# Score matmuls of two split heads issued together on four row groups, with a fourth score bank taken from the turned probabilities

## Chip, cores, metric

The kernel runs on one core of one Trainium2 chip. The metric is device time in microseconds of one execution: the median of several, compared with the kernel before on the same chip.

## What is computed

A first block (mixed attention, then a hierarchical mixture of experts) is followed by two layers of a second block, over 256 tokens of width 1024 in float32. The change concerns the two layers of the second block. Each projects its normalized input to 24 tiles of 128 columns, does three kinds of attention, gates them, and projects back:

```python
def second_block(x, mem, ...):
    for l in range(2):
        h = rms_norm_2(x, pre_norm[l]); proj = h @ w_in[l]
        # D: 6 "split" heads. Each has two halves of 32 columns with a softmax of their own
        #    p = softmax(q1 k1^T / sqrt(32)) - lam * softmax(q2 k2^T / sqrt(32));  o = p @ v
        # G: 6 heads of 64 columns on 2 key heads (normalized, rotated)
        # M: 4 heads of 64 columns against a memory of 256 rows
        y = concat([rms(o_D) * silu(gate_D), o_G * silu(gate_G), o_M * silu(gate_M)]) @ w_out[l]
        x = x + rms_norm_2(y, post_norm[l])
```

For a D head, a score matrix of 256 x 256 is computed for each half with a contraction of only 32.

## The kernel before

Every engine has a program of its own, written out in one fixed order, and they meet at semaphores. That order comes from `schedule()`: a list of turns, each of which has **jobs** and then at most one attention **step**. Jobs are the pieces beside attention: `tile2` (one 128-column tile of the input projection, 24 matmuls in three passes of a float32 product split in high and low parts, lines 851 to 853), `swap` (the pair exchange of the rotation, L1031), `vn` (a turn of values, L1027), `hsq` and `hso` (sums over a head, L1034, L1038), `y2` (output projection). Steps of a layer are D0 to D5, G0 to G5, M0 to M3.

In the turn of a step TensorE does, in this order: the step's scores (`run_scores`), the turn's jobs, for every second step the product of probabilities and values of two earlier heads (`run_out`, L1192 and L1196), and the turn (transpose) of the probabilities of the step before (`run_turn`, L1145). VectorE normalizes the step before (`norms`), takes the row maxima of this step's scores (`maxes`, L1940 for D, L1946 for G and M), and then makes the low parts of the weights that coming `tile2` jobs use (`low`, L2187) and takes jobs. ScalarE does the exponentials (`exps`, L1515 for D, L1521 for G and M), the high parts of the weights (`high`, L1572), the jobs' results out of PSUM, and the turned probabilities out of PSUM (`take_turned`, L1542). The two steps M2 and M3 at a layer's end have no projection tiles beside them; there the turn of M3's probabilities follows that of M2's.

PSUM has eight banks: score banks 0 to 2 in rotation over score jobs (`n % 3`), banks 3 and 4 in alternation for turned probabilities (`3 + n % 2`), 5 for the products with the values, 6 and 7 for jobs. A D step is two score jobs, one for each half, and so takes two banks; `s_bank(n)` waits until the exponentials of the step that had the bank last are done. A D step's four matmuls (L1104) have 32 rows of the array each: an even head's two halves lie on array rows 0 to 31 and 32 to 63, an odd head's on 64 to 95 and 96 to 127. G and M heads are already scored two at a time, on two groups of 64 rows, in the turn of the even one (L1123).

Of the kernel before, what the change touches and what calls it, by code (L numbers as in the profile page):

```python
# [11 lines left out]
ALU = mybir.AluOpType  # L12
ACT = mybir.ActivationFunctionType
X = mybir.AxisListType.X
# [279 lines left out]


S_OWNER = [n for n, s in enumerate(STEPS) for _ in range(S_JOBS[s[0]])]


def item_of(job):
# [99 lines left out]
def build(nc, ins, out):  # L399
    ctx = ExitStack()  # L400
    with ctx:
# [443 lines left out]
        def _(pe):  # L845
# [196 lines left out]

            def s_bank(n):

                if n >= 3:
                    owner = S_OWNER[n - 3]
                    if STEPS[owner][0] in "AB":
                        pe.wait_ge(maxed, owner + 1)
                    else:
                        pe.wait_ge(exped, owner + 1)  # L1050
                return bank(n % 3)

            def run_scores(step):
                kind, l, h = STEPS[step]
                n = s_first(step)
                if kind == "A":
                    for tile in (h % 2, 2):
                        from_act(("tile1", tile))
                    base = HD * (h // 2)
                    q, k = tile3[base:base + HD, h % 2, :], tile3[base:base + HD, 2, :]  # L1060
                    s = s_bank(n)
                    pe.matmul(s[:, 0:P], q[:, 0:P], k[:, 0:P], start=True, stop=True)
                    pe.matmul(s[:, P:3 * P], q[:, P:T], k[:, 0:T], start=True, stop=True).then_inc(scores, 1)
                elif kind == "C":
                    from_act(("cqt", 3))
                    pe.wait_ge(setup, 2)
                    q, k = qc3[0:C_QK, h, :], kc3[0:C_QK, h, :]
                    s = s_bank(n)
                    pe.matmul(s[:, 0:P], q[:, 0:P], k[:, 0:P], start=True, stop=False)
                    pe.matmul(s[:, 0:P], ident_b[:, :], causal_b[:, :], start=False, stop=True)  # L1070
                    pe.matmul(s[:, P:3 * P], q[:, P:T], k[:, 0:T], start=True, stop=False)
                    pe.matmul(s[:, 2 * P:3 * P], ident_b[:, :], causal_b[:, :], start=False, stop=True
                              ).then_inc(scores, 1)
                elif kind == "B":
                    for g in range(B_GROUPS):
# [12 lines left out]
                    s = s_bank(n + 1)  # L1088
                    for g in range(2):
                        q, k = qk(g)  # L1090
                        mm = pe.matmul(s[:, T * g:T * g + T], q[:, P:T], k[:, 0:T], start=True, stop=True)
                    mm.then_inc(scores, 1)
                    s = s_bank(n + 2)
                    q, k = qk(2)
                    pe.matmul(s[:, 0:T], q[:, P:T], k[:, 0:T], start=True, stop=True).then_inc(scores, 1)
                elif kind == "D":
                    pe.wait_ge(roped, max(rope_nth(l, h // 2), rope_nth(l, 3 + h // 2)))

                    banks = [s_bank(n), s_bank(n + 1)]
                    for tt in range(2):  # L1100
                        for m in range(2):
                            base = HD * (h % 2) + 32 * m
                            q, k = tile3[base:base + 32, h // 2, :], tile3[base:base + 32, 3 + h // 2, :]
                            mm = pe.matmul(banks[m][:, T * tt:T * tt + T], q[:, P * tt:P * tt + P], k,  # L1104
                                           start=True, stop=True)
                            if tt == 1:
                                mm.then_inc(scores, 1)
                elif h % 2 == 0:
                    if kind == "G":
                        pe.wait_ge(k_copied, l + 1)  # L1110
                    else:
                        from_act(("tile2", l, 20 + h // 2))
                    two = []
                    for m in range(2):
                        rows = slice(HD * m, HD * m + HD)
                        if kind == "G":
                            own = 15 if m == (h + m) // 3 else 16
                            two.append((s_bank(n + m), tile3[rows, 12 + h // 2, :], tile3[rows, own, :]))
                        else:
# [270 lines left out]
        def _(act):  # L1390
# [96 lines left out]
            def exps(step):  # L1487
# [15 lines left out]
                    op = act.activation(pr[:, 384:1152], pr[:, 384:1152], ACT.Exp, bias=n_[:, 1:2],  # L1503
                                        accum_out=s_[:, 1:2])
                elif kind == "C":
                    s = bank(b0 % 3)
# [4 lines left out]
                elif kind == "D":  # L1511
                    for m in range(2):
                        for tt in range(2):
                            c = 2 * m + tt
                            op = act.activation(pr[:, T * c:T * c + T], bank((b0 + m) % 3)[:, T * tt:T * tt + T],  # L1515
                                                ACT.Exp, bias=n_[:, c:c + 1], scale=32 ** -0.5,
                                                accum_out=s_[:, c:c + 1])
                else:
                    s = bank(b0 % 3)
# [13 lines left out]
            def take_turned(step):  # L1533
                kind = STEPS[step][0]
                w = 3 * P if kind in "ABC" else 4 * P
                for m in range(T_JOBS[kind]):
                    n = t_first(step) + m
                    if n >= 4:
                        owner = max(s for s in range(len(STEPS)) if t_first(s) <= n - 4)
                        act.wait_ge(o_ready, OUT_OF[owner] + 1)  # L1540
                    act.wait_ge(turned, n + 1)
                    act.activation(probsT[:, 512 * (n % 4):512 * (n % 4) + w], bank(3 + n % 2)[:, 0:w], ACT.Copy  # L1542
                                   ).then_inc(turned_out, 1)

            def inverse_root(dst, src, scale=1.0, bias=0.0):
# [209 lines left out]
        def _(dve):  # L1755
# [140 lines left out]
            def maxes(step):  # L1896
# [11 lines left out]

                if kind == "A":
                    dve.wait_ge(scores, b0 + 1)  # L1910
                    s = bank(b0 % 3)
# [4 lines left out]
                elif kind == "B":  # L1916
                    heads = A_HEADS + h
                    dve.wait_ge(scores, b0 + 1)
                    biased(pr[:, 0:384].rearrange("p (g t) -> p g t", g=3),
                           bank(b0 % 3)[:, 0:384].rearrange("p (g t) -> p g t", g=3),  # L1920
                           bias3[:, heads:BIAS_HEADS:B_HEADS, P - 1::-1], m_[:, 0:1])
                    dve.wait_ge(scores, b0 + 2)
                    biased(pr[:, 384:896].rearrange("p (g t) -> p g t", g=2),
                           bank((b0 + 1) % 3).rearrange("p (g t) -> p g t", g=2),
                           bias3[:, heads:heads + B_HEADS + 1:B_HEADS, ::-1], m_[:, 1:2])
                    dve.wait_ge(scores, b0 + 3)
                    link(biased(pr[:, 896:1152], bank((b0 + 2) % 3)[:, 0:T], bias3[:, heads + 2 * B_HEADS, ::-1],
                                m_[:, 2:3]))
                    link(dve.tensor_tensor(m_[:, 1:2], m_[:, 1:2], m_[:, 2:3], ALU.max))
                    dve.tensor_scalar(n_[:, 0:2], m_[:, 0:2], -1.0, None, ALU.mult).then_inc(maxed, 1)  # L1930
                elif kind == "C":
                    dve.wait_ge(scores, b0 + 1)
                    s = bank(b0 % 3)
                    dve.tensor_reduce(m_[:, 0:1], s[:, 0:P], X, ALU.max)
                    link(dve.tensor_reduce(m_[:, 1:2], s[:, P:3 * P], X, ALU.max))
                    dve.tensor_scalar(n_[:, 0:2], m_[:, 0:2], -(C_QK ** -0.5), None, ALU.mult).then_inc(maxed, 1)
                elif kind == "D":
                    for tt in range(2):
                        dve.wait_ge(scores, b0 + tt + 1)
                        op = dve.tensor_reduce(m_[:, 2 * tt:2 * tt + 2],  # L1940
                                               bank((b0 + tt) % 3).rearrange("p (m t) -> p m t", m=2), X, ALU.max)
                    link(op)
                    dve.tensor_scalar(n_[:, 0:4], m_[:, 0:4], -(32 ** -0.5), None, ALU.mult).then_inc(maxed, 1)
                else:
                    dve.wait_ge(scores, b0 + 1)
                    link(dve.tensor_reduce(m_[:, 0:2], bank(b0 % 3).rearrange("p (m t) -> p m t", m=2), X, ALU.max))  # L1946
# [420 lines left out]
```

## Time and profile before

| | us |
|---|---|
| median of 3 runs (753.81, 754.43, 759.05) | 754.43 |
| the profiled execution, its own time | 761.98 |
| its span from first to last instruction | 760.2 |
| mean granted TensorE clock of it | 0.952 of full speed |

The profile is of one execution, which was longer than the median. Rows give start and length of instructions in microseconds from the span's start. A matmul in float32 (not the split products) shows as two records. The first layer of the second block runs from about 445 us on, the second from about 597 us.

### The profile page before, as it was taken

The numbers are of one execution on the slowest core, as the hardware profiler recorded it, in microseconds if no ns is written. First come the engines' busy times: TensorE is split into PE (matmuls) and PEld (weight loads), VectorE is DVE, ScalarE is ACT, GpSimd is POOL, SyncE is SP. The second block draws the span as 40 slices with busy tenths as digits, with TensorE's granted clock in tenths as the row PEclk, the third lists the DMA queues.
The fourth block names the chain that finished last, engine by engine and source line by source line (L and its number), as shares of the span: only waits on it lengthen the run. The fifth ranks groups of instructions, "written<-read, shape, count | busy, mean of one in ns | idle before, by whom it ended". The sixth has DMA issues, their size and how long they took to land.

```text
span 760.2 us, 11653 instructions
## 1 busy us (share of the span) xinstructions
PE 682.1 (90%) x4580; PEld 520.5 (68%) x4582; DVE 368.4 (48%) x813; ACT 324.3 (43%) x759; POOL 16.8 (2%) x31
## 2 busy tenths in 40 slices
PE   6989999996599999798796799999979999999986
PEld 4968998695343455264251388878859898888876
DVE  1633657445432132021121456678775466787733
ACT  2565665421000112020120243678865545788742
POOL 5001000000000000000000000000000000000000
PEclk9999999898589999898989899999999999999999
DMA  9967331399959999999999729008163080073301
GB/s 280 340 201 246 111 112 56 123 302 367 315 223 350 414 410 414 415 409 416 414 410 411 251 88 300 1 1 274 61 221 111 1 274 5 1 231 103 111 1 56
DMA packets 94616, 167.80 MB, mean 221 GB/s; under 512 B 4238, under 2 KB 75648, under 8 KB 90464
## 3 DMA queue, kind: packets, MB, share of 16 engines
q1 hardware_dynamic: 92272, 160.88, 59.0%
q0 software_dynamic: 2160, 6.07, 2.3%
q8 instruction: 39, 0.64, 0.3%
q14 instruction: 17, 0.14, 0.1%
q10 hardware_dynamic: 128, 0.08, 0.0%
HBM read 165.93 MB, written 1.07 MB: 220 GB/s over the span
## 4 chain that ended last, share of the span: by engine, by line
PE 72%; SPq 11%; DMA 5%; ACT 5%; DVE 4%; issue 2%; ACTq 0%; DVEq 0%
PE psum L851 13%; PE psum L853 11%; PE psum L852 11%; SPq L741 9%; PE psum L1206 4%; PE psum L1247 4%; PE psum L894 4%; PE psum L1145 3%; DMA ring<-in_w_expert_down_dram 3%; PE psum L1261 3%; PE psum L1192 2%; DMA ring<-in_w_expert_up_dram 2%; PE psum L986 2%; PE psum L1104 2%; PE psum L1233 1%
## 5 line engine op out<-in xcount | busy, mean ns | idle before, releaser
L851 PE MATMUL psum<-a_high,w_high 128*128 128x256 f32 x512 | 150.9, 295 | 2.1 <-ACT q_c L1472 1.3
L853 PE MATMUL psum<-a_high,w_low 128*128 128x256 f32 x512 | 144.7, 283 | 0.0
L852 PE MATMUL psum<-x_low,w_high 128*128 128x256 f32 x512 | 144.6, 283 | 0.0
L2187 DVE TENSOR_TENSOR w_low<-ring,w_high 128x1024 fp32r<-128x1024 f32 (+1 forms) x79 | 111.2, 1421 | 23.4 <-ACT w_high L1572 23.3
L851 PEld LDWEIGHTS psum<-a_high,w_high 128*128 128x128 f32 x512 | 97.7, 191 | 13.8 <-issue 4.7
L1572 ACT ACTIVATE w_high<-ring 128x1024 fp32r<-128x1024 f32 (+1 forms) x79 | 95.9, 1219 | 9.6 <-DMA ring<-in_w_in_dram 6.2
L852 PEld LDWEIGHTS psum<-x_low,w_high 128*128 128x128 f32 x512 | 97.8, 191 | 0.4
L853 PEld LDWEIGHTS psum<-a_high,w_low 128*128 128x128 f32 x512 | 97.8, 191 | 0.0
L851 PE MATMUL psum<-w_high,a_high 128*128 128x256 f32 x240 | 69.6, 290 | 0.0
L852 PE MATMUL psum<-w_low,a_high 128*128 128x256 f32 x240 | 68.5, 285 | 0.0
L1247 PE MATMUL psum<-ring,q_c 128*32 128x512 f32 x320 | 55.1, 682 | 11.0 <-DMA ring<-in_w_expert_up_dram 7.0
L1206 PEld LDWEIGHTS psum<-tiles,x_nat 128*128 128x128 f32 x256 | 55.2, 307 | 9.1 <-issue 9.1
L1206 PE MATMUL psum<-tiles,x_nat 128*128 128x128 f32 x256 | 56.9, 382 | 2.1 <-DVE tiles L2104 2.1
L853 PE MATMUL psum<-w_high,mix_low 128*128 128x256 f32 x192 | 54.8, 286 | 0.0
L2115 DVE TENSOR_SCALAR tiles<-tiles 128x256 f32<-128x256 f32 x8 | 2.3, 292 | 101.2 <-ACT tiles L1620 101.2
L851 PEld LDWEIGHTS psum<-w_high,a_high 128*128 128x128 f32 x240 | 46.7, 195 | 3.2 <-issue 2.3
L852 PEld LDWEIGHTS psum<-w_low,a_high 128*128 128x128 f32 x240 | 46.8, 195 | 0.0
L1620 ACT ACTIVATE tiles<-psum 128x256 f32<-128x256 f32 x8 | 3.1, 383 | 97.1 <-PE psum L1247 97.1
L1247 PEld LDWEIGHTS psum<-ring,q_c 128*32 128x32 f32 x320 | 13.6, 123 | 42.5 <-issue 42.5
L853 PEld LDWEIGHTS psum<-w_high,mix_low 128*128 128x128 f32 x192 | 37.4, 195 | 0.0
L1614 ACT ACTIVATE q_c<-psum 128x512 f32<-128x512 f32 x16 | 9.6, 597 | 62.7 <-PE psum L1206 62.7
L1145 PE MATMUL psum<-const,probs 128*128 128x128 f32 x200 | 32.2, 283 | 4.5 <-DVE probs L1973 2.4
(334 smaller groups left out, 1190.4 us busy)
## 6 DMA issues: line engine op xcount, KB each, us to landing
ring<-in_w_in_dram SPq DMA_DIRECT2D x36, 1024.0 KB, 8.7
ring<-in_w_expert_down_dram SPq DMA_DIRECT2D x24, 1024.0 KB, 18.0
ring<-in_w_expert_gate_dram SPq DMA_DIRECT2D x40, 512.0 KB, 14.6
ring<-in_w_expert_up_dram SPq DMA_DIRECT2D x40, 512.0 KB, 15.3
ring<-in_w_out_dram SPq DMA_DIRECT2D x12, 1024.0 KB, 5.1
ring<-in_w_mem_kv_dram SPq DMA_DIRECT2D x4, 1024.0 KB, 16.5
k_c<-in_w_expert_gate_dram SPq DMA_DIRECT2D x5, 512.0 KB, 14.9
k_c<-in_w_expert_up_dram SPq DMA_DIRECT2D x5, 512.0 KB, 15.9
```

Source lines behind the costliest of these rows:

```text
L741: sp.dma_start(to[:, SLOT // 2 * m:SLOT // 2 * m + SLOT // 2].rearrange("p (k n) -> p k n", n=DE), w[:, 4 * half:4 * half + 4, :]).then_in ...
L851: pe.matmul(dst, left[0], right[0], start=first, stop=False)
L852: pe.matmul(dst, left[0], right[1], start=False, stop=False)
L853: return pe.matmul(dst, left[1], right[0], start=False, stop=last)
L894: mm = pe.matmul(dst, src[:, k, P * tt:P * tt + P], w[:, k, a:b], start=(k == 0), stop=(k == KC - 1))
L986: mm = pe.matmul(dst[:, 0:T], w[:, k, P * n:P * n + P], memT[l][:, k, :], start=(k == 0), stop=(k == KC - 1))
L1145: mm = pe.transpose(dst[:, P * c:P * c + P], pr[:, a:a + P], ident)
L1206: mm = pe.matmul(dst[:, P * c:P * c + P], x[:, k, :], places2[:, tt, :], start=(tt == 0), stop=(tt == 1))
L1247: mm = pe.matmul(bank(6)[PLACES * e:PLACES * e + PLACES, :], gathered2[b % 2][:, k, PLACES * e:PLACES * e + PLACES], w, start=(k == 0), st ...
L1261: mm = pe.matmul(bank((7, 5)[half])[PLACES * e:PLACES * e + PLACES, :], hiddenT[:, k, PLACES * e:PLACES * e + PLACES], expert_slot(n)[:, a ...
L1572: act.activation(split_like_raw(n)[0], raw_of(n), ACT.Copy).then_inc(highs, 1)
L2187: dve.tensor_tensor(w_l, raw_of(n), as_f32(w_h), ALU.subtract).then_inc(lows, 1)
```

## The change

In both later layers, the scores of D heads h and h+1 are issued together in the turn of even h: eight matmuls on four groups of 32 array rows, each group with a score bank of its own; odd D steps issue none. The score banks of these layers rotate over four (0 to 3), and bank 4 alone holds turned probabilities, so that each `run_turn` there waits until the turned probabilities before it have been copied out, where it waited for those before the last. The waits of VectorE and ScalarE stay as they were; the banks that they read follow `s_at` and `t_at`. Nothing changes in the first block.

```diff
+LATER = STEP[("D", 0, 0)]
+def s_at(n):
+    first = s_first(LATER)
+    return n % 3 if n < first else (n - first) % 4
+S_BEFORE = {n: max((m for m in range(n) if s_at(m) == s_at(n)), default=None) for n in range(len(S_OWNER))}
+def t_at(n):
+    return 3 + n % 2 if n < t_first(LATER) else 4
...
             def s_bank(n):
-                if n >= 3:
-                    owner = S_OWNER[n - 3]
+                if S_BEFORE[n] is not None:
+                    owner = S_OWNER[S_BEFORE[n]]
...
                 elif kind == "D":
-                    pe.wait_ge(roped, max(rope_nth(l, h // 2), rope_nth(l, 3 + h // 2)))
-                    banks = [s_bank(n), s_bank(n + 1)]
-                    for tt in range(2):
-                        for m in range(2):
-                            base = HD * (h % 2) + 32 * m
-                            q, k = tile3[base:base + 32, h // 2, :], tile3[base:base + 32, 3 + h // 2, :]
+                    if h % 2 == 0:
+                        pe.wait_ge(roped, max(rope_nth(l, h // 2), rope_nth(l, 3 + h // 2)))
+                        banks = [s_bank(n + m) for m in range(4)]
+                        for tt in range(2):
+                            for m in range(4):
+                                q, k = (tile3[32 * m:32 * m + 32, at + h // 2, :] for at in (0, 3))
...
-                    if n >= 2:
+                    if n > t_first(LATER):
+                        pe.wait_ge(turned_out, n)
+                    elif n >= 2:
                         pe.wait_ge(turned_out, n - 1)
-                    dst = bank(3 + n % 2)
+                    dst = bank(t_at(n))
```

On TensorE, where head D2 opens a pair (turn of D0's probabilities, L1145, then the scores, L1104, then a projection tile), before:

```order
L1145 MATMUL psum<-const,probs 128x128 [waits turned_out,normed]
L1145 MATMUL psum<-const,probs 128x128 x3
L1104 MATMUL psum<-tiles 128x256 [waits exped,roped]
L1104 MATMUL psum<-tiles 128x256 x3
L851 MATMUL psum<-a_high,w_high 128x256 [waits lows,p_act]
```

and now, with line numbers some 15 higher:

```order
L1162 MATMUL psum<-const,probs 128x128 [waits turned_out,normed]
L1162 MATMUL psum<-const,probs 128x128 x3
L1119 MATMUL psum<-tiles 128x256 [waits exped,roped]
L1119 MATMUL psum<-tiles 128x256 x7
L866 MATMUL psum<-a_high,w_high 128x256 [waits lows,p_act]
```

The same place holds eight score matmuls instead of four, behind waits of the same names. On TensorE at head D3, between the turn of D1's probabilities and the rotation's exchange (L1031), before:

```order
L1034 MATMUL psum<-q_c,const 128x256 [waits squared,p_act]
L1145 MATMUL psum<-const,probs 128x128 [waits turned_out,normed]
L1145 MATMUL psum<-const,probs 128x128 x3
L1104 MATMUL psum<-tiles 128x256 [waits exped,roped]
L1104 MATMUL psum<-tiles 128x256 x3
L1031 MATMUL psum<-tiles,const 128x256 [waits p_act]
L851 MATMUL psum<-a_high,w_high 128x256 [waits lows,p_act]
```

and now:

```order
L1049 MATMUL psum<-q_c,const 128x256 [waits squared,p_act]
L1162 MATMUL psum<-const,probs 128x128 [waits turned_out,normed]
L1162 MATMUL psum<-const,probs 128x128 x3
L1046 MATMUL psum<-tiles,const 128x256 [waits p_act]
L866 MATMUL psum<-a_high,w_high 128x256 [waits lows,p_act]
```

The score matmuls and their waits are gone from D3, as from D1 and D5, in both layers: six places. On every other engine the instructions and the names of their waits stand as before.

## Rows read from the trace of the kernel before

**Rows 1.** The page: span, and TensorE's busy time.

```profile
span 760.2 us, 11653 instructions
PE 682.1 (90%) x4580; PEld 520.5 (68%) x4582; DVE 368.4 (48%) x813; ACT 324.3 (43%) x759; POOL 16.8 (2%) x31
```

**Rows 2.** Busy time by stretch (microseconds busy, instructions; then clock, DMA share, GB/s).

```profile
466.00:520.00 54.00, 52.44 (x396) 45.56 (x395) 42.39 (x96) 35.21 (x95) 0.00 (x0) 1.00 0.27 84
567.00:573.00 6.00, 4.86 (x28) 3.56 (x29) 2.88 (x3) 3.39 (x4) 0.00 (x0) 0.72 0.00 0
626.00:675.00 49.00, 47.52 (x361) 41.22 (x359) 36.65 (x83) 33.34 (x93) 0.00 (x0) 1.00 0.20 63
```

**Rows 3.** Waits, 466 to 520: TensorE's two, one of VectorE (total, times, longest).

```profile
PE psum L1034 <- ACT tiles L1458: 0.9, 2, 0.6
PE psum L1027 <- ACT tiles L1458: 0.6, 1, 0.6
...
DVE small L1940 <- PE psum L1104: 8.5, 3, 3.4
```

**Rows 4.** Timeline of TensorE around head D1's scores (start, length).

```profile
480.55 0.28 PE L852 MATMUL psum<-x_low,w_high 128*128 128x256 f32 x1
480.67 0.28 PE L853 MATMUL psum<-a_high,w_low 128*128 128x256 f32 x1
480.88 1.13 PE L1104 MATMUL psum<-tiles 32*128 32x256 f32 x8
481.94 0.38 PE L851 MATMUL psum<-a_high,w_high 128*128 128x256 f32 x1
482.17 0.28 PE L852 MATMUL psum<-x_low,w_high 128*128 128x256 f32 x1
```

**Rows 5.** Timeline of TensorE around head D5's scores.

```profile
510.38 0.60 PE L1034 MATMUL psum<-q_c,const 128*128 128x256 f32 x2
510.82 0.60 PE L1145 MATMUL psum<-const,probs 128*128 128x128 f32 x4
511.35 1.13 PE L1104 MATMUL psum<-tiles 32*128 32x256 f32 x8
512.41 0.70 PE L1031 MATMUL psum<-tiles,const 128*128 128x256 f32 x2
```

**Rows 6.** Line 1104 alone (ns min/median/max), and its part within 480.8 to 481.0.

```profile
L1104 PE MATMUL psum<-tiles x96: 374/374/478, 473.4 to 666.3; 32*128 32x256 f32 x96
...
480.88 0.48 PE L1104 MATMUL psum<-tiles 32*128 32x256 f32 x2
```

**Rows 7.** Timeline of TensorE, an expert's last product, four column groups of 32.

```profile
301.43 0.64 PE L1261 MATMUL psum<-ring,tiles 128*32 128x512 f32 x4 [0.51 <-ACT tiles L1625]
...
301.43 3.21 PE L1261 MATMUL psum<-ring,tiles 128*32 128x512 f32 x28 [0.51 <-ACT tiles L1625]
```

**Rows 8.** Timeline of VectorE at D1 and D2, and TensorE's product at 493.64.

```profile
479.28 0.88 DVE L1967 SCALAR_TENSOR_TENSOR probs<-probs,small 128x256 f32<-128x256 f32 x2
482.04 1.29 DVE L1940 TENSOR_REDUCE small<-psum 128x2 f32<-128x512 f32 x2 [1.88 <-PE psum L1104]
...
492.17 1.22 DVE L2187 TENSOR_TENSOR w_low<-ring,w_high 128x1024 fp32r<-128x1024 f32 x1
...
493.64 0.28 PE L851 MATMUL psum<-a_high,w_high 128*128 128x256 f32 x1
```

**Rows 9.** Timeline of ScalarE after head D3's scores, and TensorE behind it.

```profile
501.28 0.47 ACT L1515 ACTIVATE probs<-psum,small 128x256 f32<-128x256 f32 x1 [1.61 <-DVE small L1943]
...
503.10 1.07 ACT L1572 ACTIVATE w_high<-ring 128x1024 fp32r<-128x1024 f32 x1
504.04 0.39 ACT L1456 ACTIVATE q_c<-psum 128x256 f32<-128x256 f32 x1
...
504.85 0.70 PE L1034 MATMUL psum<-q_c,const 128*128 128x256 f32 x2 [0.24 <-ACT tiles L1458]
```

**Rows 10.** Timeline at the second layer's end: M2's copy, M3's normalization and turn.

```profile
725.54 0.60 ACT L1542 ACTIVATE probsT<-psum 128x512 f32<-128x512 f32 x1 [0.19 <-PE psum L1145]
725.85 0.35 DVE L1973 TENSOR_SCALAR probs<-probs,small 128x256 f32<-128x256 f32 x1
726.26 0.66 PE L1145 MATMUL psum<-const,probs 128*128 128x128 f32 x4 [0.81 <-DVE probs L1973]
```

More of the change, by code:

```diff
@@ L1050, in s_bank @@
                         pe.wait_ge(exped, owner + 1)
-                return bank(n % 3)
+                return bank(s_at(n))
             def run_scores(step):
@@ L1096, in run_scores @@
                 elif kind == "D":
-                    pe.wait_ge(roped, max(rope_nth(l, h // 2), rope_nth(l, 3 + h // 2)))
-                    banks = [s_bank(n), s_bank(n + 1)]
-                    for tt in range(2):
-                        for m in range(2):
-                            base = HD * (h % 2) + 32 * m
-                            q, k = tile3[base:base + 32, h // 2, :], tile3[base:base + 32, 3 + h // 2, :]
[L1104 to L1107, printed above, removed]
+                    if h % 2 == 0:
[4 more added lines that the diff above has]
+                                q, k = (tile3[32 * m:32 * m + 32, at + h // 2, :] for at in (0, 3))
+                                mm = pe.matmul(banks[m][:, T * tt:T * tt + T], q[:, P * tt:P * tt + P], k,
+                                               start=True, stop=True)
+                                if tt == 1:
+                                    mm.then_inc(scores, 1)
                 elif h % 2 == 0:
@@ L1505, in exps @@
                 elif kind == "C":
-                    s = bank(b0 % 3)
+                    s = bank(s_at(b0))
                     sc = C_QK ** -0.5
@@ L1514, in exps @@
                             c = 2 * m + tt
-                            op = act.activation(pr[:, T * c:T * c + T], bank((b0 + m) % 3)[:, T * tt:T * tt + T],
+                            op = act.activation(pr[:, T * c:T * c + T], bank(s_at(b0 + m))[:, T * tt:T * tt + T],
                                                 ACT.Exp, bias=n_[:, c:c + 1], scale=32 ** -0.5,
@@ L1518, in exps @@
                 else:
-                    s = bank(b0 % 3)
+                    s = bank(s_at(b0))
                     for tt in range(2):
@@ L1541, in take_turned @@
                     act.wait_ge(turned, n + 1)
-                    act.activation(probsT[:, 512 * (n % 4):512 * (n % 4) + w], bank(3 + n % 2)[:, 0:w], ACT.Copy
+                    act.activation(probsT[:, 512 * (n % 4):512 * (n % 4) + w], bank(t_at(n))[:, 0:w], ACT.Copy
                                    ).then_inc(turned_out, 1)
@@ L1910, in maxes @@
                     dve.wait_ge(scores, b0 + 1)
-                    s = bank(b0 % 3)
+                    s = bank(s_at(b0))
                     biased(pr[:, 0:P], s[:, 0:P], bias3[:, h, P - 1::-1], m_[:, 0:1])
@@ L1919, in maxes @@
                     biased(pr[:, 0:384].rearrange("p (g t) -> p g t", g=3),
-                           bank(b0 % 3)[:, 0:384].rearrange("p (g t) -> p g t", g=3),
+                           bank(s_at(b0))[:, 0:384].rearrange("p (g t) -> p g t", g=3),
                            bias3[:, heads:BIAS_HEADS:B_HEADS, P - 1::-1], m_[:, 0:1])
@@ L1923, in maxes @@
                     biased(pr[:, 384:896].rearrange("p (g t) -> p g t", g=2),
-                           bank((b0 + 1) % 3).rearrange("p (g t) -> p g t", g=2),
+                           bank(s_at(b0 + 1)).rearrange("p (g t) -> p g t", g=2),
                            bias3[:, heads:heads + B_HEADS + 1:B_HEADS, ::-1], m_[:, 1:2])
                     dve.wait_ge(scores, b0 + 3)
-                    link(biased(pr[:, 896:1152], bank((b0 + 2) % 3)[:, 0:T], bias3[:, heads + 2 * B_HEADS, ::-1],
+                    link(biased(pr[:, 896:1152], bank(s_at(b0 + 2))[:, 0:T], bias3[:, heads + 2 * B_HEADS, ::-1],
                                 m_[:, 2:3]))
@@ L1932, in maxes @@
                     dve.wait_ge(scores, b0 + 1)
-                    s = bank(b0 % 3)
+                    s = bank(s_at(b0))
                     dve.tensor_reduce(m_[:, 0:1], s[:, 0:P], X, ALU.max)
@@ L1940, in maxes @@
                         op = dve.tensor_reduce(m_[:, 2 * tt:2 * tt + 2],
-                                               bank((b0 + tt) % 3).rearrange("p (m t) -> p m t", m=2), X, ALU.max)
+                                               bank(s_at(b0 + tt)).rearrange("p (m t) -> p m t", m=2), X, ALU.max)
                     link(op)
@@ L1945, in maxes @@
                     dve.wait_ge(scores, b0 + 1)
-                    link(dve.tensor_reduce(m_[:, 0:2], bank(b0 % 3).rearrange("p (m t) -> p m t", m=2), X, ALU.max))
+                    link(dve.tensor_reduce(m_[:, 0:2], bank(s_at(b0)).rearrange("p (m t) -> p m t", m=2), X, ALU.max))
                     dve.tensor_scalar(n_[:, 0:2], m_[:, 0:2], -(HD ** -0.5), None, ALU.mult).then_inc(maxed, 1)
```

## The prediction

> **What bounds the kernel now.** I read the page first: TensorE is busy 682.1 us of a span of 760.2 us, the other engines under half of it [rows 1]. A share over the whole span says little of one stage, so I then asked for the stretches in which the D heads lie, 466 to 520 us and 626 to 675 us. There TensorE is busy 52.44 of 54 us and 47.52 of 49 us, at full clock; VectorE is at 42.39, ScalarE at 35.21, DMA at 0.27 and 0.20 of its engines [rows 2]. The waits of the first stretch show what the missing 1.5 us are: TensorE waited 0.9 us at two head sums and 0.6 us at a turn of values, each time for ScalarE to take a result that TensorE had just made [rows 3]. It never waits there for weights, for probabilities or for a score bank. The reverse is seen: VectorE waited 8.5 us, three times, for the D scores [rows 3]. So in these stretches TensorE's own queue sets the time, and what is taken from it comes off the end, as long as no other engine becomes late for it.
>
> **Term 1: the six score blocks that go.** A D step shows as eight records of L1104 (four matmuls, two records each). What one block costs the queue is read from starts, not from lengths, since matmuls overlap. Around D1: product matmuls follow each other every 0.12 us (480.55, 480.67); the L853 before the block starts at 480.67 and the L852 two places behind it at 482.17 [rows 4]. Without the block they would be 0.24 apart, so it costs 482.17 - 480.67 - 0.24 = 1.26 us. Around D5: four transposes last 0.60 us from 510.82 and one alone about 0.27, so they start 0.11 apart and the next instruction could start at 511.26. The exchange L1031 starts at 512.41 and lasts 0.70 where the like L1034 without a change of shape ahead of it lasts 0.60 [rows 5]. Cost: 512.41 - 511.26 + 0.10 = 1.25 us. Both give the same; I take 1.255. Six blocks (D1, D3, D5, in two layers): 6 x 1.255 = **7.53 us off**.
>
> **Term 2: the six blocks that double.** What an eight-record block is made of decides what sixteen cost. Two records start together at 480.88 and last 0.48; of the 96 the median is 0.374, the longest 0.478 [rows 6]. So the first pair carries 0.10 us of weight load, and the block's 1.13 us are 0.10 + three steps + 0.37, a step being (1.13 - 0.10 - 0.37) / 3 = 0.22 us. Hence four rounds of two at 0.22 (0.86 us), and 1.255 - 0.86 = 0.39 us for going in and out. Each round is two row groups at once. With four groups on four banks, sixteen records are again four rounds if four run as well as two do. The trace has no four row groups, so the bounds are these. Lowest: no row gives a reason for a block to get shorter, so the cost is at least nothing. The nearest row is the experts' last product: four matmuls on four column groups start together (x4 in 0.64 us) and 28 of them take 3.21 us, so a round of four takes (3.21 - 0.64) / 6 = 0.43 us for 512 columns, or 0.215 for 256 [rows 7]: the same as the round of two above. So four at a time can be issued and kept up. Highest: rows that are only like it by number, and not by group kind, can't exclude that all sixteen run one after another, 16 x 0.22 = 3.46 us. I take four rounds, since two row groups and four column groups both do it, and add 0.014 us a block for the third and fourth start: 6 x 0.014 = **0.08 us on**.
>
> **Term 3: waits that shift.** Of every wait on the D path I asked who would be late if TensorE comes 1.25 us earlier for each block gone.
> - D1: VectorE finished D0's normalization at 480.16 and then stood 1.88 us until D1's scores, its maxima starting at 482.04 [rows 8]. These scores will have been there since D0. So maxima, and the low weights behind them, come 1.88 us earlier against 1.25 us for TensorE. Nothing is lost.
> - D2: the low part of a tile starts at 492.17 and ends at 493.39, and its product starts at 493.64 [rows 8]. That is 0.25 us of room, but both hang on the D2 block, so both move together. A doubled block that delays the first banks beyond its own end is not in sight.
> - D3: ScalarE stood 1.61 us before D3's exponentials because the maxima hung on the scores; the weight split behind them starts at 503.10 and pushes the take of a tile (504.04), and TensorE waits 0.24 us at the head sum at 504.85 [rows 9]. With D3's scores already there, ScalarE starts when it is free. It was free at 501.28 - 1.61 = 499.67, a moment that moves with D1's block but not with D3's; against the TensorE work behind D3 that is 499.67 + 1.255 = 500.92, or 0.36 us earlier than 501.28. So the take comes up to 0.36 us earlier and most of the 0.24 us wait goes: 2 layers x 0.2 = **0.4 us off** (at most 2 x 0.24).
> - Score banks: D2 and D4 wait for D1's and D3's exponentials, as before; G and M steps wait for an older owner than before.
> - The one bank of turned probabilities: `run_turn` now waits for ScalarE's copy of the step before. In the D and G stretch that copy lies a whole projection tile (24 x 0.12 = 2.9 us) ahead. The tight place is the layer's end: in the second layer M2's copy ends at 725.54 + 0.60 = 726.14, M3's normalization at 725.85 + 0.35 = 726.20, and the turn starts at 726.26, released by the latter [rows 10]. So the new wait ends 0.06 us before the old one does: cost nothing. If that cover went, it would cost at most the copy's 0.60 us, once a layer.
> - DMA issues are not moved, and the weight loads have room at 0.27 and 0.20 [rows 2].
>
> **Sum.** -7.53 + 0.08 - 0.4 = -7.85 us. The profiled execution took 761.98 us, so the like of it would take 754.1; that is 7.55 us over the median of 754.43. The blocks of the sum run at full clock in either, so the absolute saving carries over: 754.43 - 7.85 = **746.6 us**, -1.04%. A measurement of this kernel can tell about 1% (7.5 us) from no change, and the forecast lies on that edge.
>
> A rule of the Trainium skill speaks against part of term 2. The page "TensorE: Matmul & The Clock Gate", section "Measured speedup vs the span model", gives 3.07x for four row tiles of 32, not four. By it sixteen records would take 3.46 / 3.07 = 1.13 us instead of 0.86, and the sum would be an estimated 1.6 us less. The rounds of rows 6 and 7 show no such loss, and the sum goes by them.
>
> **Rivals.**
> - *Four row groups don't quite run as four.* If two of the four weight loads in a round don't hide (0.10 us, the load ahead of the first pair [rows 6]) in three rounds, a block grows by 0.31 us: 6 x 0.31 = 1.9 us back, 748.5 us. For it: no row of four row groups. Against it: rows 7. The page's 3.07 above would give nearly this.
> - *Only two row groups run at a time.* Eight rounds: a block costs 8 x 0.216 + 0.39 = 2.12 us, a pair saves only the second way in and out, 0.39 us. 6 x 0.39 = 2.3 us off, 752.1 us. The order written in the code (all four of one half of the queries, then the other) speaks against it, with rows 7.
> - *Slower: the four groups run one after another.* A block costs 3.46 + 0.39 = 3.85 us where two cost 2.51, 6 x 1.34 = 8.0 us on: 762.4 us. It decides from the point at which a round of four takes over (2.51 - 0.39) / 4 = 0.53 us, against 0.22 shown. Against it: pairs that overlap fully.
> - *The clock at a layer's end.* From 567 to 573 us the clock is at 0.72 on average [rows 2]: with full speed as 1 and 0.5 as the lower level, 1.2 GHz of 2.4, that is 3.4 us at the lower, after the waits among the last heads. It costs some 1.7 us. The end is no shorter now, but the products behind it may meet one such stretch more or less: 748.3 or 744.9 us.
> - *The change doesn't do what it says.* The order shows eight matmuls at three places a layer and none at the other three, so I leave this no chance.
>
> **Chances.** Forecast 0.70, four not quite as four 0.11, two at a time 0.07, clock 0.09 (half each way), one after another 0.03. Range 744.0 to 751.0: it holds the forecast with the scatter of the three runs, the first rival and the clock, and leaves out the second and the third. Faster by over 1% means below 746.9: six tenths of the forecast's 0.70 and half of the clock's, 0.46. Slower by over 1%: 0.03. Within: 0.51.
>
> **What would show it.** Right: L1119 with 96 records in six blocks of 16, four starting within 0.03 us, each block about 1.14 us long and the next instruction 1.07 us after its start; D1, D3, D5 with the tile or the exchange right behind the transposes; VectorE's waits for D scores in the first layer down from three (8.5 us) to D2's alone, of some 3 to 5 us; no new wait of L1162 for the copy L1542's successor. Wrong: blocks of 1.5 us or more (first two rivals), a gap of TensorE ahead of a product because of VectorE's low part, or of L1162 in the D and G stretch because of ScalarE's copy.

## The result, and the profile after

| | before | changed |
|---|---|---|
| median of 20 runs each, same chip | 758.51 | 754.89 |
| profiled execution: its time | 761.98 | 754.51 |
| its span | 760.2 | 752.7 |
| its mean granted clock | 0.952 | 0.960 |

The ratio, taken round by round, is 0.9942 with a 95% interval of [0.992, 0.9965]: 4.4 us less, between 2.7 and 6.1 (the two medians alone lie 3.6 apart). One execution of the changed kernel, of 1591.68 us, is left out of the comparison. Two things parted from the forecast of 746.6. The saving is smaller than 7.85 us, and the kernel before, whose three runs had a median of 754.43, has one of 758.51 over twenty.

The page of the changed kernel, to set beside [rows 1]:

```profile
span 752.7 us, 11653 instructions
PE 670.2 (89%) x4580; PEld 515.5 (68%) x4582; DVE 368.3 (49%) x813; ACT 324.7 (43%) x759; POOL 16.8 (2%) x31
```

TensorE is busy 11.9 us less in the same 4580 records, 6.8 of it the six blocks of 1.13 us. The sum is no measure of the change: two more profiles of the changed kernel read 671.8 and 666.6 us. The spans differ by 7.5 us, part of which lies outside the changed stretch. The clean measure is the distance between two products of the same tiles. First the doubled block, by line (compare [rows 6]) and in the timeline of TensorE at D0 and at D2 (start, length, operation, what ended the idle time):

```profile
L1119 PE MATMUL psum<-tiles x96: 374/374/478, 470.5 to 654.4; 32*128 32x256 f32 x96
...
470.45 1.15 PE L1119 MATMUL psum<-tiles 32*128 32x256 f32 x16
471.53 0.48 PE L1046 MATMUL psum<-tiles,const 128*128 128x256 f32 x1
...
484.86 0.60 PE L1162 MATMUL psum<-const,probs 128*128 128x128 f32 x4
485.39 1.15 PE L1119 MATMUL psum<-tiles 32*128 32x256 f32 x16
486.46 0.38 PE L866 MATMUL psum<-a_high,w_high 128*128 128x256 f32 x1
```

Sixteen records take 1.15 us where eight took 1.13 [rows 4], and the next instruction starts 1.07 or 1.08 us after the block where it was 1.06. Each single record is as long as before (374 ns). So four row groups with a bank each do run as four.

Now the path, as starts of the first product of projection tiles in the order in which they are made, from TensorE's timeline (line 851 before, 866 after), first layer. The head's block that the change took away stands in the second column.

| from tile to tile | holds | before | changed | difference |
|---|---|---|---|---|
| 0 to 6 | | 22.30 | 22.33 | |
| 6 to 8 | D1 | 7.09 | 5.94 | -1.15 |
| 8 to 16 | (D2) | 8.73 | 8.65 | -0.08 |
| 16 to 13 | D3 | 9.33 | 8.57 | -0.76 |
| 13 to 14 | (D4) | 7.32 | 6.75 | -0.57 |
| 14 to 17 | D5 | 5.66 | 5.65 | -0.01 |
| 17 to 18 | (G0) | 9.42 | 9.42 | 0 |
| 0 to 18 | | 69.86 | 67.31 | -2.55 |

Its end rows, the first product of tiles 0 and 18, of the kernel before:

```profile
452.55 0.47 PE L851 MATMUL psum<-a_high,w_high 128*128 128x256 f32 x1
...
522.41 0.47 PE L851 MATMUL psum<-a_high,w_high 128*128 128x256 f32 x1
```

and of the changed kernel:

```profile
449.54 0.47 PE L866 MATMUL psum<-a_high,w_high 128*128 128x256 f32 x1
...
516.85 0.47 PE L866 MATMUL psum<-a_high,w_high 128*128 128x256 f32 x1
```

The second layer reads 69.84 and 67.31. So the trace shows 5.1 us, which lies in the measured interval. D1 gave what was forecast (its last 0.1 us lies in the next row, where the first products of tile 8 no longer follow a block), D5 gave nothing. The timeline of TensorE in D5's turn, compare [rows 5]:

```profile
504.83 0.60 PE L1049 MATMUL psum<-q_c,const 128*128 128x256 f32 x2
505.27 0.60 PE L1162 MATMUL psum<-const,probs 128*128 128x128 f32 x4
506.62 0.70 PE L1046 MATMUL psum<-tiles,const 128*128 128x256 f32 x2 [0.75 <-ACT tiles L1475]
507.43 0.38 PE L866 MATMUL psum<-a_high,w_high 128*128 128x256 f32 x1
```

The block is gone from between the transposes and the exchange, and a wait for ScalarE stands in its place. ScalarE's timeline there says what it was doing:

```profile
503.05 0.48 ACT L1532 ACTIVATE probs<-psum,small 128x256 f32<-128x256 f32 x1 [1.61 <-DVE small L1960]
...
504.87 1.06 ACT L1589 ACTIVATE w_high<-ring 128x1024 fp32r<-128x1024 f32 x1
505.81 0.39 ACT L1473 ACTIVATE q_c<-psum 128x256 f32<-128x256 f32 x1
506.08 0.49 ACT L1475 ACTIVATE tiles<-psum,vecs 128x256 f32<-128x256 f32 x1
506.43 0.50 ACT L1488 ACTIVATE q_c<-psum,small 128x256 f32<-128x256 f32 x1
506.96 0.42 ACT L1489 ACTIVATE q_c<-q_c 128x256 f32<-128x256 f32 x1
```

ScalarE does D4's exponentials, splits a weight chunk (1.06 us), and only then takes tile 14 out of its bank, until 506.57; the exchange, which writes that bank, starts at 506.62. The take of the head sum ends at 507.38, and product 17, which writes the bank of the sum, starts at 507.43. The same engines in the kernel before, ScalarE's two takes:

```profile
511.63 0.49 ACT L1458 ACTIVATE tiles<-psum,vecs 128x256 f32<-128x256 f32 x1
...
512.52 0.42 ACT L1472 ACTIVATE q_c<-q_c 128x256 f32<-128x256 f32 x1
```

and TensorE's D4 block and product 17:

```profile
505.92 1.13 PE L1104 MATMUL psum<-tiles 32*128 32x256 f32 x8
...
512.99 0.39 PE L851 MATMUL psum<-a_high,w_high 128*128 128x256 f32 x1
```

There the take of tile 14 ended at 512.12, 0.29 us ahead of the exchange at 512.41 [rows 5], and the head sum's take at 512.94, 0.05 us ahead of product 17. These two are not alike. The exchange of the changed kernel, which did wait, starts 0.05 us after the take's end as well (506.57 and 506.62), so 0.05 us is no room at all. Product 17 starts 0.58 us behind the exchange, where after D4's block, with nothing to wait for, a product follows its exchange after 0.35 (506.98 and 507.33): it already waited some 0.24 us for ScalarE in the kernel before. The view lists no wait because the exchange, 0.70 us long, covers it. The exchange itself had 0.24 us to spare. From the start of D4's scores to product 17 it is 512.99 - 505.92 = 7.07 us before, and 507.43 - 500.36 = 7.07 us after, with the scores' start read from this row of the changed kernel's timeline:

```profile
500.36 1.15 PE L1119 MATMUL psum<-tiles 32*128 32x256 f32 x16
```

The two are equal because product 17 ends the same chain in both: from D4's scores over VectorE's maxima and ScalarE's queue to the head sum's take. That chain was already 0.24 us longer than TensorE's own work.

The waits of the first stretch, TensorE's and one of VectorE, against [rows 3]:

```profile
PE psum L1046 <- ACT tiles L1475: 0.8, 1, 0.8
PE psum L1042 <- ACT tiles L1475: 0.6, 1, 0.6
PE psum L1049 <- ACT tiles L1475: 0.6, 1, 0.6
...
DVE small L1957 <- PE psum L1119: 4.5, 2, 3.9
```

The 0.24 us wait at the head sum before D4 is gone, the exchange's is new. One more is too short to be listed. In D3's turn:

```profile
494.30 0.60 PE L1046 MATMUL psum<-tiles,const 128*128 128x256 f32 x2
495.03 0.39 PE L866 MATMUL psum<-a_high,w_high 128*128 128x256 f32 x1
```

Product 13 starts 0.73 us behind the exchange, where it was 0.34 (499.66 and 500.00 before). ScalarE's L1489 ran from 494.57 to 494.99 there, and product 13 starts 0.04 later. Again D3's block had covered it: 0.39 us of it came back as a wait. This one is read from the timeline and from the bank that product 13 shares with that head sum; no run below takes it away.

### The profile page after: what moved, and what is told of

Read it like the earlier page. It is cut to its first block, busy times and chain, and to the rows that moved or that the text cites. A ratio compares the mean times of both kernels' runs of the same rounds, so it can differ in the third digit from the quotient of the medians.

```text
span 752.7 us, 11653 instructions
## 1 busy us (share of the span) xinstructions
PE 670.2 (89%) x4580; PEld 515.5 (68%) x4582; DVE 368.3 (49%) x813; ACT 324.7 (43%) x759; POOL 16.8 (2%) x31
## 3 DMA queue, kind: packets, MB, share of 16 engines
HBM read 165.93 MB, written 1.07 MB: 222 GB/s over the span
## 4 chain that ended last, share of the span: by engine, by line
PE 70%; SPq 15%; ACT 6%; DVE 4%; DMA 3%; issue 2%; ACTq 0%; DVEq 0%
PE psum L866 13%; SPq L756 12%; PE psum L868 12%; PE psum L867 12%; PE psum L909 4%; PE psum L1264 4%; PE psum L1223 3%; PE psum L1162 3%; PE psum L1209 2%; PE psum L1278 2%; PE psum L1001 2%; SPq L759 2%; DMA values<-in_w_expert_up_dram 2%; PE psum L1250 1%; PE psum L1138 1%
## 5 line engine op out<-in xcount | busy, mean ns | idle before, releaser
L1264 PE MATMUL psum<-ring,q_c 128*32 128x512 f32 x320 | 51.7, 645 | 13.4 <-DMA ring<-in_w_expert_up_dram 9.3
```

The source lines that it names most:

```text
L1264: mm = pe.matmul(bank(6)[PLACES * e:PLACES * e + PLACES, :], gathered2[b % 2][:, k, PLACES * e:PLACES * e + PLACES], w, start=(k == 0), st ...
```

## Experiments

All ratios are against the kernel before on the same chip, five rounds each. "0 to 18" is the distance of the table above, first and second layer. The theory after the comparison, A: *the exchange and product 17 in D5's turn hang on ScalarE, so D5's block was cover and is worth nothing.* Rival B: *the saving is small because banks rotate otherwise, or because four groups at once cost something.* Rival C: *the missing part is the clock.*

**The changed kernel again**, to see the scatter.

> The changed kernel again, on the chip of the next three. It gives their difference, and how much the low stretches of the clock vary. My reading of the two traces: from the first tile of a layer (first product of tile 0) to the scores of G0 and G1 it takes 65.9 us in either layer, where the kernel before takes 68.4 to 68.5, so about 5.1 us in two layers, ratio 0.993. The rest of a difference between two profiles is the clock.

Measured: 0.9916 [0.9883, 0.9949], 752.75 us against 759.06. 0 to 18: 67.29 and 67.30. The intervals within the layer repeat to 0.02 us, while the median ratio moved by 0.26 points between two series: the distances tell more than the medians.

**The banks alone.** Four rotating score banks and one bank of turned probabilities, but every head scored in its own turn.

```diff
+JOINT = ()
-                    if h % 2 == 0:
+                    own = range(4) if h in JOINT else range(2 * (h % 2), 2 * (h % 2) + 2)
+                    if h in JOINT or h - 1 not in JOINT:
-                        banks = [s_bank(n + m) for m in range(4)]
+                        banks = {m: s_bank(n + m - own[0]) for m in own}
-                            for m in range(4):
+                            for m in own:
```

> Only the banks of the change: score jobs of the later layers rotate over four banks, turned probabilities have bank 4 alone, and each D head is scored in its own turn as in the kernel before. My theory (all of the gain comes from the blocks at D1 and D3, the one bank for turned probabilities costs nothing at full clock): tile 0 to tile 18 takes 69.85 us in both layers as before, ratio 1.000. Rival (the single bank eats a part of the gain): a turn of probabilities that waits for ScalarE's copy, and up to 0.6 us more at each layer's end, ratio 1.001 to 1.002.

Measured: 0.9999 [0.9978, 1.0019]; 0 to 18: 69.87 and 69.86, as before the change. The banks cost nothing and give nothing. B's first half falls. Its second half falls by the blocks of sixteen records, after which the next instruction starts 1.07 or 1.08 us after their start, against 1.06 behind eight: 0.02 us a block.

**The last pair apart**: `JOINT = (0, 2)`, so that D4 and D5 are scored each in its turn again.

> D0 with D1 and D2 with D3 are scored together, D4 and D5 each in its own turn, on four banks as in the change. Theory A (behind the pair D4/D5 ScalarE's chain is late: four exponentials, a weight split of 1.06 us, then the take of tile 14, for which the exchange in D5's turn waits, so D5's block was cover and its removal saves nothing): tile 0 to G0 stays at 65.9 us, and the 0.75 us wait of the exchange goes because the block stands there again. Theory B (the saving is lost elsewhere, each block gone being worth the same third of it): tile 0 to G0 gets 0.85 us longer, 66.75 us. Forecast's theory (each block 1.25 us): 67.2 us.

Measured: 0.9938 [0.9907, 0.9968]; 0 to 18: 67.28 and 67.28, the same as with all three pairs joined. TensorE's timeline in D5's turn of this kernel:

```profile
502.56 0.60 PE L1164 MATMUL psum<-const,probs 128*128 128x128 f32 x4
503.09 1.13 PE L1121 MATMUL psum<-tiles 32*128 32x256 f32 x8
504.16 0.70 PE L1047 MATMUL psum<-tiles,const 128*128 128x256 f32 x2
504.74 0.39 PE L867 MATMUL psum<-a_high,w_high 128*128 128x256 f32 x1
```

A block of 1.13 us is put back and costs nothing: product 17 starts 2.18 us after the transposes, and 2.16 with the wait in the block's place. This is the strongest run for A.

**The last pair alone**: `JOINT = (4,)`.

> Only D4 with D5 is scored together; D0 to D3 each in its own turn. Theory A: nothing is gained over the kernel before, tile 0 to G0 68.4 us, with a wait of the exchange of about 0.7 us in D5's turn; ratio 1.000. Theory B: 0.85 us a layer gained, 67.6 us. The forecast's: 67.2 us, ratio 0.9967.

Measured: 1.0 [0.9965, 1.0034]; 0 to 18: 69.87 and 69.87. The timeline shows the wait in place of the block:

```profile
507.48 0.60 PE L1164 MATMUL psum<-const,probs 128*128 128x128 f32 x4
508.82 0.70 PE L1047 MATMUL psum<-tiles,const 128*128 128x256 f32 x2 [0.75 <-DVE w_low L2206]
509.63 0.39 PE L867 MATMUL psum<-a_high,w_high 128*128 128x256 f32 x1
```

A lesson in reading: here the releaser named is VectorE's low part, which ended at the same moment. The exchange waits for nothing of VectorE's (in the program its one wait is `p_act`, ScalarE's takes). The next run decides which it is.

**ScalarE's weight split behind the takes.** In the changed kernel, the split that ScalarE makes ahead of tile 14's take (it is for tile 18) is done after the take of head sum 13; VectorE's low parts stay where they are.

```diff
-                    for n in SPLIT_AT.get(j, ()):
+                    late = job[0] == "tile2" and job[2] == 14
+                    for n in () if late else SPLIT_AT.get(j, ()):
                         high(n)
...
+                    if job[0] == "hsq" and job[2] == 13:
+                        for n in SPLIT_AT.get(JOB[("tile2", job[1], 14)], ()):
+                            high(n)
```

> The change, and in the turn of D4 ScalarE makes the 1.06 us weight split (high part for the tile after next but one) after it has taken tile 14 and head sum 13, not before. TensorE's order is untouched. Theory A: the exchange in D5's turn waits 0.1 us or less instead of 0.75 and product 17 starts some 0.8 us earlier: tile 0 to G0 65.1 us, 1.6 us less in two layers than the changed kernel, ratio to before 0.991. Rival (the trace names VectorE's low part, which ends at the same instant, as what released the exchange in the second layer): VectorE's low part stays where it is, so the wait stays, 65.9 us.

Measured: 0.9914 [0.989, 0.9938]; 0 to 18: 66.52 and 66.66. The exchange no longer shows a wait, and 14 to 17 is 4.87 us in place of 5.65. Product 17 still hangs on the head sum's take: it starts 0.81 us behind the exchange, where 0.34 would do. But 18 to 20 grew from 4.74 to 5.40 (and in the second layer 17 to 18 from 9.42 to 9.55). The waits of this kernel and the row behind them:

```profile
PE psum L866 <- DVE w_low L2208: 1.0, 1, 1.0
...
519.32 0.35 PE L866 MATMUL psum<-a_high,w_high 128*128 128x256 f32 x1 [1.01 <-DVE w_low L2208]
```

So 0.78 us came off up to tile 18 and 0.66 went back at tile 20. Its weights' high part had long been made, from 509.68 to 510.74. It is VectorE that came late with the low part: it had first stood 0.58 us for ScalarE's sigmoid of a gate tile (`k_c`), and all that follows up to the low part takes as long as in the changed kernel:

```profile
515.14 0.43 DVE L2226 TENSOR_TENSOR tiles<-tiles,k_c 128x256 f32<-128x256 f32 x1 [0.58 <-ACT k_c L1502]
...
517.95 1.22 DVE L2208 TENSOR_TENSOR w_low<-ring,w_high 128x1024 fp32r<-128x1024 f32 x1
```

This product of the gate starts 1.22 us after product 18, where in the changed kernel it is 0.57 (517.42 and 516.85): ScalarE's queue had not moved up with TensorE. The ScalarE part of A is shown (VectorE's low parts were not touched, and the wait left); as a gain it was a miss.

**The same late split in the kernel before**, where D5's block is in its place.

> The kernel before, with ScalarE's weight split in D4's turn made after its takes. If D5's block was cover for ScalarE's late take, moving the split alone brings nothing: tile 0 to tile 18 stays 69.85 us. If the order on ScalarE was a cost of its own, up to 0.8 us less in each layer.

Measured: 1.0017 [0.9985, 1.0049]; 0 to 18: 69.73 and 69.75, so 0.1 us a layer. I had expected nothing, and the exchange indeed gains nothing. But product 17 gains what it had silently waited:

```profile
510.56 0.70 PE L1031 MATMUL psum<-tiles,const 128*128 128x256 f32 x2
510.90 0.47 PE L851 MATMUL psum<-a_high,w_high 128*128 128x256 f32 x1
```

It follows the exchange after 0.34 us in place of 0.58, and 14 to 17 is 5.43 us in place of 5.66. Of these 0.23 us, 0.09 come back before tile 18. The times, with an interval of 0.3% either way, can't show this; the distances do, in both layers.

**Two splits late**, the next one of ScalarE's (that of tile 9's turn) put behind the gates of D5's turn as well.

```diff
-                    late = job[0] == "tile2" and job[2] == 14
+                    late = job[0] == "tile2" and job[2] in (14, 9)
...
+                    if what[0] == "D" and what[2] == 5:
+                        for n in SPLIT_AT.get(JOB[("tile2", what[1], 9)], ()):
+                            high(n)
```

> The fourth kernel (ScalarE's split in D4's turn after its takes) saved 0.78 us up to product 17 and gave 0.66 us back before product 20, whose low part waits on VectorE for the gates that ScalarE had not done. Theory: ScalarE is back to back from D4's exponentials to G0's, and its next split (in D5's turn, between the takes of tiles 17 and 9) is what now delays the gates. Here that split too is made later, after the gates of D5's turn. Expected: product 17 as in the fourth kernel, product 20 0.66 us earlier against it: tile 0 to product 20 71.3 us, where the changed kernel takes 72.05; 1.5 us less in two layers, ratio to before 0.991. Rival: VectorE's own queue is the limit there, and product 20 stays where it is, 72.0 us.

Measured: 0.9908 [0.9874, 0.9943]; tiles 0 to 20: 71.24 and 71.25, where the changed kernel has 72.05. So tile 20 is back at 4.74 us behind tile 18, and the 0.78 us stay. The waits of the first layer show neither the exchange nor tile 20's product:

```profile
PE psum L1042 <- ACT tiles L1475: 0.6, 1, 0.6
PE psum L1049 <- ACT tiles L1475: 0.6, 1, 0.6
```

**A bank of its own for M3's turned probabilities**: the score bank of M0, free by then.

```diff
+    for l in range(LAYERS):
+        if n == t_first(STEP[("M", l, 3)]):
+            return s_at(s_first(STEP[("M", l, 0)]))
...
-                    if n > t_first(LATER):
-                        pe.wait_ge(turned_out, n)
-                    elif n >= 2:
-                        pe.wait_ge(turned_out, n - 1)
+                    if n >= 2:
+                        pe.wait_ge(turned_out, t_free(n))
```

> The change, but the turned probabilities of M3, the last head of a layer, go into the score bank that M0 had, so that this turn waits neither for ScalarE's copy of M2's nor for anything new. In the changed kernel that turn waited 0.8 us for the copy in the one layer end where the clock was at its lower level, and for VectorE's normalization where it was not. Expected: no wait of that turn for ScalarE at either clock; a layer's end shorter by at most 0.3 us with the clock low, 0 otherwise; not to be seen in the time.

Measured: 0.99 [0.9862, 0.9939]; 0 to 18: 67.29 and 67.28. The reason for the run: at the first layer's end the changed kernel's turn waited for ScalarE's copy, as its waits from 554 to 567 us say:

```profile
PE psum L1162 <- ACT probsT L1559: 0.8, 1, 0.8
```

With a bank of its own the turn never waits for the copy, and the layer's end gets no shorter: tile 20 to the output projection takes 44.06 us against 43.96. The two profiles have different lower-clock stretches there, so this doesn't resolve a few tenths; in the changed kernel VectorE's normalization, for which the turn waits as well, ended at 560.93 + 0.35 = 561.28, and the copy at 561.43, with the turn at 561.57. So at most 0.15 us of the 0.8 was the bank's.

**All of it**: two splits late, M3's own bank, and D0's probabilities turned ahead of the turn of values `vn` 7, where TensorE waited 0.6 us at L1042.

```diff
+                    if job[0] == "vn" and job[2] == 7:
+                        run_turn(step - 1)
                     run(job, j)
...
-                    if not opens(step):
+                    if not opens(step) and what[0::2] != ("D", 1):
                         run_turn(step - 1)
```

> The changed kernel with what the runs so far point to: ScalarE's two weight splits later, M3's turned probabilities in a bank of their own, and on TensorE the turn of D0's probabilities ahead of the last values turn (vn 7) of D1's turn, which waits 0.62 us for ScalarE's take of tile 15. Four transposes are 0.44 us of work that fits into that wait. Expected by layer: product 16 starts 0.4 us earlier against product 8, tile 0 to product 20 70.8 us (changed kernel 72.05, two splits later 71.25); in two layers 2.4 us less than the changed kernel, 7.5 less than before, ratio to before 0.990. Rival: something on VectorE or ScalarE takes the 0.44 us back before product 12, whose low part had 0.27 us of room: then product 12 or 13 starts no earlier.

Measured: 0.9882 [0.9841, 0.9922], 750.0 us against 759.74, the lowest median of all versions. 8 to 16 fell from 8.65 to 8.21, tiles 0 to 20 are 70.80 and 70.82. The timeline at the place moved:

```profile
481.20 0.60 PE L1172 MATMUL psum<-const,probs 128*128 128x128 f32 x4
481.98 0.44 PE L1054 MATMUL psum<-const,tiles 128*128 128x128 f32 x2 [0.18 <-ACT tiles L1487]
482.35 1.15 PE L1131 MATMUL psum<-tiles 32*128 32x256 f32 x16
```

The transposes lie where 0.62 us of waiting were, and 0.18 are left.

**The changed kernel on that chip.**

> The changed kernel a third time, on the chip of the one before it: tile 0 to product 20 72.05 us; ratio to before 0.993, and the combined kernel 2.4 us faster than it, which the scatter of the times (some 7 us from end to end) will hardly resolve.

Measured: 0.9932 [0.9906, 0.9957], 754.58 us; 0 to 18: 67.30 and 67.31. By the distances the version above is 2.5 us faster than the changed kernel (72.05 - 70.80, in two layers); the two intervals overlap, so the times alone don't prove it.

## Why the prediction missed

**What bounds the kernel** was right as far as TensorE's queue goes, and wrong in "as long as no other engine becomes late": I read the waits that there were, and not how late the next releaser was where there was none.

**Term 1 (7.53 us off) failed, at D5 and in part at D3.** The failed step is the overlap: the term takes each block at its full price for TensorE's queue, as if nothing behind it waited for another engine. The price of 1.255 us holds where that is so: D1 gave 1.15 + 0.08 a layer, and D2's doubled block took 0.02 of it. At D3, turn to product 13, TensorE's stretch fell from 500.00 - 498.06 = 1.94 to 495.03 - 493.86 = 1.17 us, so 0.77 and not 1.16, since 0.39 came back at product 13. At D5 the block gave 0.01 us a layer in place of 1.255. [Rows 5] end with the very exchange (L1031) that came to wait, and I never asked when its bank was free. The answer stood in the trace of before: 0.24 us of room at the exchange, and at product 17 none, since it was already held up by 0.24 us. The runs with the last pair apart and alone show this from both sides, and the late split, in the changed kernel and in the one before, shows that the chain runs through ScalarE. For D3's 0.39 us the cause is read from the timeline alone.

**Term 2 (0.08 on) was right.** The blocks measure 0.02 us more each. Rivals one to three (four not quite four, two at a time, one after another) fall by the blocks of 1.15 us. The Trainium skill's 3.07x for four row tiles ("TensorE: Matmul & The Clock Gate", "Measured speedup vs the span model") gave an estimated 0.27 us more for a block, so 1.4; no run here shows that loss.

**Term 3 (0.4 off) was too small where it looked, and blind beside it.** ScalarE's earlier take gave 0.51 us a layer between tiles 13 and 14, where I had allowed 0.24 at most: from the turn of values to the head sum it is 0.27 us and was 0.68 (504.17 to 504.85 before), and the head sum is 0.10 shorter when it need not wait. The 0.24 listed counts from the end of the instruction before, and the distance between starts was 0.41 too long. (The rest of the 0.57 is 0.08 at the first product of tile 13, where D3's block is gone, less 0.02 for D4's doubled block.) The 0.39 at product 13 is of the kind that I looked for and did not find.

By layer, the forecast was 3.92 us and the trace shows 2.55: D5 is 1.25 short, D3 0.4, the doubled blocks 0.03, and term 3 gave 0.31 more than forecast. That the total is not further off is in part luck, since this last error goes the other way.

**The copy and VectorE's waits.** The single bank of turned probabilities cost nothing in the banks-only run, as forecast. At the first layer's end with the clock low the turn did wait 0.8 us for ScalarE's copy, the wait that I had bounded at 0.60; taking it away made that end no shorter within what its profiles resolve. VectorE's waits for D scores fell from 8.5 us in three to 4.5 in two: D2's of 3.9, as forecast, and 0.6 at D4, which the forecast had at nothing.

**The base.** My 754.43 was a median of three that lay 4 us under that of twenty. The relative forecast, -1.04%, against -0.58% measured, misses by the saving alone; 0.9942 x 754.43 would be 750.1 us, inside the range. With the base of twenty runs and the forecast saving it would be 750.7, inside as well. It took both errors to leave the range; only the saving is the mechanism's. The profiled execution, 7.55 us over that median, had hinted at the base, and I put it down to that one execution.

**The clock rival** was real but goes by execution, not by kernel. Busy times and granted clock (the last column but two) from 558 to 570 us, changed kernel as first profiled:

```profile
558.00:570.00 12.00, 9.82 (x47) 7.33 (x48) 5.42 (x11) 6.12 (x10) 0.00 (x0) 0.57 0.11 38
```

and its second profile:

```profile
558.00:570.00 12.00, 8.14 (x63) 6.74 (x64) 6.29 (x15) 7.32 (x15) 0.00 (x0) 1.00 0.16 55
```

The same program went through the first layer's end with some 10 us at the lower clock once (12 x (1 - 0.57) / 0.5 = 10.3) and with none once. From tile 18 to the next layer's first tile it took 48.70 + 37.28 us and 47.87 + 35.61 us: 2.5 us apart, half of what the change brought. Why the clock falls in one execution and not in another stays open. Of the 7.5 us between the two first spans, 3.0 lie ahead of the changed code (452.55 against 449.54 at tile 0) and belong to no part of the change. C falls as the cause of the missing saving, since that is missing in a stretch at full clock.

## What to carry to other kernels

Before counting a block that leaves the bound engine's queue, go to every instruction behind it that waits for something, waits for a bank of two jobs earlier included, and read when its releaser ended: the room there, and not the block's length, is what the removal can bring. A gap of 0.05 us is not room: here it is what lies between a releaser's end and the start of what waited for it. And an instruction that starts before the one ahead has ended can wait without any wait being listed; the distance between their starts, against the same pair elsewhere, shows it (0.58 against 0.34 us here). When the chain through the helper engine is shortened too, follow that engine's queue to its next customer: the first late split gave 0.78 us and lost 0.66 at tile 20, because VectorE stood for a result that ScalarE still made as late as before; it took the second late split to keep the gain.

## What the runs showed of the hardware

Matmuls of 32 rows on four row groups with four banks, sixteen records, take 1.15 us, where two groups with eight take 1.13: the other two groups come for 0.02 us. And the lower-clock stretches at the same place of the same program vary between none and some 10 us from one execution to the next, worth 2.5 us here.
